# Two of eight K-tile pairs of a feed-forward input by seven block products instead of eight

## What is computed

```python
h = rms_norm(x, ffn_pre_g[l])
gate, up = jnp.split(h @ w_ffn_in[l], 2, axis=-1)
x = x + rms_norm((jax.nn.silu(gate) * up) @ w_ffn_out[l], ffn_post_g[l])
```

## Time and profile before

| | us |
|---|---|
| median of 3 runs (lowest, highest) | 2449.61 (2449.6, 2450.51) |
| span of the profiled execution | 2448.3 |
| one unit of 12 matmuls in the feed-forward input | 2.72 |
| one pair of loop bodies with its transposes | 88.44 |

### The profile page before, as it was taken

One profiled execution on the slowest core, in us unless ns is written; L12 is line 12 of the kernel. 1 busy time (PEld: TensorE's weight loads), 2 busy tenths in 40 slices (PEclk: granted clock), 3 DMA queues, 4 the chain that ended last, 5 costly groups with the idle time before them and its releaser, 6 DMA issues.

```text
span 2448.3 us, 32568 instructions
## 1 busy us (share of the span) xinstructions
PE 2432.0 (99%) x12315; PEld 2031.6 (83%) x12315; DVE 1396.9 (57%) x1987; ACT 1203.4 (49%) x1693; POOL 37.0 (2%) x60
## 2 busy tenths in 40 slices
PE   9999999999999999999999999999999999999998
PEld 7888888887888888888887889898888888888887
DVE  5568888677455555454446436677554554554444
ACT  5665558666444444444345435554544444443443
POOL 1000000000000000000000010000000000000000
PEclk9999999999999999999999999999999999999999
DMA  7765544445655655555556764434555556556554
GB/s 235 243 209 179 167 148 172 165 170 182 197 189 188 195 188 189 191 189 191 196 191 204 220 217 156 143 113 164 180 190 190 189 188 195 189 188 206 194 193 154
DMA packets 233850, 455.80 MB, mean 186 GB/s; under 512 B 16698, under 2 KB 19002, under 8 KB 233232
## 3 DMA queue, kind: packets, MB, share of 16 engines
q1 hardware_dynamic: 227008, 431.49, 54.3%
q0 software_dynamic: 6160, 21.81, 2.6%
q10 hardware_dynamic: 576, 1.05, 0.1%
HBM read 449.04 MB, written 5.24 MB: 186 GB/s over the span
## 4 chain that ended last, share of the span: by engine, by line
PE 96%; DVE 2%; ACT 1%; DMA 1%; issue 0%; SPq 0%; ACTq 0%; DVEq 0%
PE g L312 24%; PE g L314 24%; PE g L313 24%; PE g L1326 4%; PE g L1327 4%; PE g L1328 4%; PE g L2263 1%; PE g L2267 1%; PE g L2265 1%; PE m L829 1%; PE m L1358 1%; PE m L2276 1%; DVE wl L300 1%; PE m L1041 0%; PE m L2348 0%
## 5 line engine op out<-in xcount | busy, mean ns | idle before, releaser
L300 DVE TENSOR_TENSOR wl<-raw,wh 128x1024 fp32r<-128x1024 f32 (+1 forms) x820 | 996.0, 1220 | 920.7 <-ACT wh L296 917.0
L296 ACT ACTIVATE wh<-raw 128x1024 fp32r<-128x1024 f32 (+1 forms) x819 | 860.4, 1056 | 1066.9 <-PE g L314 911.3
L312 PE MATMUL g<-wh,act_hi 128*128 128x512 f32 x1792 | 702.0, 392 | 0.9 <-DVE wl L300 0.5
L314 PE MATMUL g<-wh,act_lo 128*128 128x512 f32 x1792 | 697.7, 389 | 0.0
L313 PE MATMUL g<-wl,act_hi 128*128 128x512 f32 x1792 | 697.4, 389 | 0.0
L312 PEld LDWEIGHTS g<-wh,act_hi 128*128 128x128 f32 x1792 | 336.4, 188 | 73.6 <-issue 2.9
L314 PEld LDWEIGHTS g<-wh,act_lo 128*128 128x128 f32 x1792 | 336.3, 188 | 70.5
L313 PEld LDWEIGHTS g<-wl,act_hi 128*128 128x128 f32 x1792 | 336.5, 188 | 68.7
L312 PE MATMUL g<-wh,ht_hi 128*128 128x512 f32 x672 | 261.6, 389 | 0.0
L314 PE MATMUL g<-wh,ht_lo 128*128 128x512 f32 x672 | 261.4, 389 | 0.0
L313 PE MATMUL g<-wl,ht_hi 128*128 128x512 f32 x672 | 261.4, 389 | 0.0
(11 more groups left out here) (424 smaller groups left out, 2225.6 us busy)
## 6 DMA issues: line engine op xcount, KB each, us to landing
raw<-in_w_ffn_in SPq DMA_DIRECT2D x176, 512.0 KB, 3.5
raw<-in_ffn_w_in SPq DMA_DIRECT2D x176, 512.0 KB, 3.5
raw<-in_w_in SPq DMA_DIRECT2D x111, 512.0 KB, 4.5
raw<-in_w_ffn_out SPq DMA_DIRECT2D x88, 512.0 KB, 3.5
raw<-in_ffn_w_out SPq DMA_DIRECT2D x88, 512.0 KB, 3.6
raw<-in_nsa_w_in SPq DMA_DIRECT2D x80, 512.0 KB, 4.4
raw<-in_w_out SPq DMA_DIRECT2D x32, 512.0 KB, 4.1
raw<-in_nsa_w_out SPq DMA_DIRECT2D x32, 512.0 KB, 4.6
```

The source lines that it names most:

```text
L296: nc.scalar.activation(wh[:, j % SLOTS, 0:n], raw[:, j % SLOTS, 0:n], ACT.Copy).then_inc(hi_done, 1)
L300: nc.vector.tensor_tensor(wl[:, j % SLOTS, 0:n], raw[:, j % SLOTS, 0:n], wh[:, j % SLOTS, 0:n].bitcast(F32), ALU.subtract).then_inc(lo_don ...
L312: nc.tensor.matmul(dst, h, whk, start=(first and k == 0), stop=False)
L314: ins = nc.tensor.matmul(dst, l, whk, start=False, stop=(last and k == 1))
```

## The change

Take two K-tiles of the gate and of the up chunk and the two halves of the rows: that is a product of a 2 x 2 matrix of activation blocks with a 2 x 2 matrix of weight blocks, eight block products. Strassen's scheme (in Winograd's form) needs seven, of sums of blocks. The changed kernel does this for K-tile pairs 1 and 2 of the eight, in every body but the first.

- A body has 20 units in the ring instead of 16 (`FF_NEXT`). Units 2 to 5 and 10 to 13 are a group of seven each (`SEVEN_AT`). Of the four units of a group two are loaded (gate and up of the pair), and two are sums that VectorE writes into the raw slots in three steps (`weight_sums`) before it converts the first unit of the group; no load is issued for them. Of a group's second unit only half is converted. TensorE runs 6, 3, 6 and 6 matmuls on them (`pe_seven`).
- The sums of activations are made once for each layer in the first body, by VectorE in five steps behind unit 11, and split by ScalarE behind unit 12 and VectorE behind unit 13.
- The products of the groups that more than one result needs stand in the four banks of `m`. ScalarE copies one out behind its unit 17, and VectorE adds them up in three steps behind its unit 17 (`shared_sums`), each of which waits for the one before. At the end of a body VectorE adds to the gate banks what is shared (`ff_b`), and ScalarE makes `silu` of that; behind unit 3 of the next body VectorE makes the up rows (`up_rows`) and then the product.
- `m` also takes the transposes. They move from behind unit 7 of an even body to behind unit 16, and TensorE waits for the shared sums before unit 16. The copies out of `m` move from behind unit 11 to the end of the body.
- Units 0, 1, 6 to 9 are the gate's other six pairs, 14 to 19 the up's.
- `g_b` is used for `shared` in the feed-forward input, so GpSimd's load of `ffn_post_g` moves to the end of it.
- Some semaphores are merged: the transpose of the gains waits for three small loads more; a wait for these is left out later.

```diff
...
+SEVENS = 2
+FF_FIRST, FF_NEXT = 16, 20
...
+        GATES, SEVEN_AT, SEVEN_K = {0: 0, 1: 3, 6: 4, 7: 5, 8: 6, 9: 7}, (2, 10), (1, 2)
+        UPS = {14: 3, 15: 4, 16: 0, 17: 5, 18: 6, 19: 7}
+
+        STEPS = {"t2": (1, 3), "rows": 2, "u2": 4, "u34": 5, "shared": 6}
...
+        def pe_seven(pe, name, i, p):
...
+            first, last = p == 0, p == SEVENS - 1
+            converted(0)
+            product(0, 0, *of_x(0, 0), m[:, 0, :], first, last)
+            product(0, 1, *of_x(1, 0), g[:, 0, :], False, last).then_inc(unit_used, 1)
+            converted(1)
+            if first:
+                pe.wait_ge(pair_free[1], s["pair0"][1] + i + 1)
+            product(1, 1, *of_sums(3), g[:, 2, :], first, False).then_inc(unit_used, 1)
+            converted(2)
+            product(2, 0, *of_sums(0), m[:, 2, :], first, last)
+            product(2, 1, *of_sums(2), m[:, 1, :], first, last).then_inc(unit_used, 1)
+            converted(3)
+            product(3, 0, *of_sums(1), m[:, 3, :], first, last)
+            product(3, 1, *of_x(1, 1), g[:, 1, :], False, last).then_inc(unit_used, 1)
...
+            def body(i, par, first):
+                if first:
+                    return opening()
+                for j in range(FF_NEXT):
+                    if j == 0:
+                        pe.wait_ge(pair_free[0], s["pair0"][0] + i + 1)
+                    if j == SEVEN_AT[0]:
+                        if par:
+                            pe.wait_ge(lo_evac, BANKS[name] + 2 * i - 2)
+                        else:
+                            pe.wait_ge(ff_step, ff_stepped(name, i - 1, STEPS["shared"]))
+                    if j == 16 and par == 0:
+                        pe.wait_ge(ff_step, ff_stepped(name, i, STEPS["shared"]))
                         pe.wait_ge(lo_evac, BANKS[name] + 2 * i - 4)
...
+                    if j in SEVEN_AT:
+                        pe_seven(pe, name, i, SEVEN_AT.index(j))
...
+                    if j == 16 and par == 0:
                         pe_ff_turn2(pe)
...
+                for j in range(FF_NEXT):
+                    if j - 1 in SEVEN_AT:
...
+                        nc.scalar.activation(wh[:, j % SLOTS, NB:UE], raw[:, j % SLOTS, NB:UE], ACT.Copy).then_inc(hi_done, 1)
+                    else:
+                        act_unit(act, ff_cyc(s, i), j)
+                    if j == 17:
+                        act.wait_ge(unit_used, ff_used(s, i, 13))
+                        nc.scalar.activation(shared[:, 0, :], m[:, 0, :], ACT.Copy).then_inc(ff_kept, 1)
+                if par == 0:
+                    act_ff_turn2(act, name, i)
+                act.wait_ge(pair_free[0], s["pair0"][0] + i + 2)
+                gated(par, 0)
+                gated(par, 1).then_inc(ff_kept, 1)
...
+            def weight_sums(i, p):
...
+                nc.vector.tensor_tensor(t1_t3, b12_b22, raw[:, j % SLOTS:j % SLOTS + 2, 0:NB], ALU.add).then_inc(raw_full[(j + 2) % SLOTS], 16)
+                dve.wait_ge(raw_full[(j + 2) % SLOTS], (cyc + (j + 2) // SLOTS) * 16 + 16)
+                nc.vector.tensor_tensor(t2_t4[:, 0, :], t1_t3[:, 0, :], b12_b22[:, 1, :], ALU.add).then_inc(ff_step, 1)
+                dve.wait_ge(ff_step, ff_stepped(name, i, STEPS["t2"][p]))
+                nc.vector.tensor_tensor(t2_t4[:, 1, :], t2_t4[:, 0, :], b11_b21[:, 1, :], ALU.add).then_inc(raw_full[(j + 3) % SLOTS], 16)
...
+            def up_rows(i):
+
+                dve.wait_ge(unit_used, ff_used(s, i, FF_NEXT - 1))
+                nc.vector.tensor_tensor(shared[:, T:2 * T, :], g[:, T:2 * T, :], shared[:, T:2 * T, :], ALU.subtract).then_inc(pair_free[1], 1)
+                dve.wait_ge(pair_free[1], s["pair0"][1] + i + 2)
...
+            def shared_sums(i):
...
+                nc.vector.tensor_tensor(shared[:, 3, :], shared[:, 0, :], m[:, 3, :], ALU.add).then_inc(ff_step, 1)
+                dve.wait_ge(ff_step, ff_stepped(name, i, STEPS["u2"]))
+                u2 = shared[:, 3:4, :].broadcast_to([P, 2, NB])
+                nc.vector.tensor_tensor(shared[:, 1:3, :], m[:, 1:3, :], u2, ALU.add).then_inc(ff_step, 1)
+                dve.wait_ge(ff_step, ff_stepped(name, i, STEPS["u34"]))
+                nc.vector.tensor_tensor(shared[:, 3, :], shared[:, 1, :], m[:, 2, :], ALU.add).then_inc(ff_step, 1)
...
+                for j in range(FF_NEXT):
+                    if j in SEVEN_AT:
+                        weight_sums(i, SEVEN_AT.index(j))
+                    if j - 1 in SEVEN_AT:
+                        half_unit(i, j)
+                    else:
+                        dve_unit(dve, ff_cyc(s, i), j)
+                    if j == 3:
+                        up_rows(i - 1)
                         mul(i - 1, 1 - par)
...
+                    if j == 17:
+                        shared_sums(i)
+                if par == 0:
+                    dve.wait_ge(turned, BANKS[name] + 2 * i)
+                nc.vector.tensor_tensor(ff_b[par][:, :, :], g[:, 0:T, :], shared[:, 0:T, :], ALU.add).then_inc(pair_free[0], 1)
+                if par == 0:
+                    dve_ff_turn2(dve, name, i)
...
         def pe_other_gains(pe):
-            pe.wait_ge(gains_in, 16 * 5)
+            pe.wait_ge(tables_in, 16 * 8)
...
-            pool.wait_ge(pair_free[1], gemms["co"]["pair0"][1] + 3)
+            pool.wait_ge(ff_step, ff_stepped("ff1", PAIRS, 1))
             pool.dma_start(g_b[:, :], bcast(a["ffn_post_g"], D)).then_inc(gb_in, 16)
...
```

More of the change, by code:

```diff
@@ new lines, in pe_ff_unit @@
+        def pe_ff_unit(pe, cyc, j, c, u, starts, last):
+            pe.wait_ge(lo_done, SLOTS + (cyc + j // SLOTS) * SLOTS + j % SLOTS + 1)
+            for k in range(2):
+                whk = wh[:, j % SLOTS, k * NB:(k + 1) * NB]
+                wlk = wl[:, j % SLOTS, k * NB:(k + 1) * NB]
+                for t in range(T):
+                    dst = g[:, 2 * c + t, :]
+                    h = act_hi[:, 2 * u + k, t * P:(t + 1) * P]
+                    l = act_lo[:, 2 * u + k, t * P:(t + 1) * P]
+                    nc.tensor.matmul(dst, h, whk, start=(t in starts and k == 0), stop=False)
+                    nc.tensor.matmul(dst, h, wlk, start=False, stop=False)
+                    ins = nc.tensor.matmul(dst, l, whk, start=False, stop=(last and k == 1))
+            ins.then_inc(unit_used, 1)
@@ L1091, in act_ffn_in, with gated @@
             s = gemms[name]
-            def body(i, par, first):
[L1094 to L1106, removed]
+            def gated(par, t):
+                src = ff_b[par] if par is not None else g
+                return nc.scalar.activation(ff_b[par or 0][:, t, :], src[:, t, :], ACT.Silu, scale=rstd(turn)[:, t:t + 1])
@@ new lines, in split_sums, with opening @@
+            def split_sums():
+                dve.wait_ge(ff_summed, 3 * LAYER[name] + 2)
+                nc.vector.tensor_tensor(sums_lo[:, :, :, :], sums[:, :, :, :], sums_hi[:, :, :, :].bitcast(F32), ALU.subtract)\
+                  .then_inc(ff_summed, 1)
+                dve.wait_ge(ff_summed, 3 * LAYER[name] + 3)
+                link_d(dve, nc.vector.memset(shared[:, T:2 * T, :], 0.0))
+            def opening():
+                if turn not in SPLIT:
+                    dve_add_block(dve, turn, 0)
+                for j in range(FF_FIRST):
+                    if j >= AHEAD:
+                        dve_unit(dve, s["u0"] // SLOTS, j)
+                    dve_lead_in(dve, turn, j)
+                    if j == 11:
+                        sums_of_x()
+                    if j == 13:
+                        split_sums()
@@ L1118, in mul @@
                                                          in1=ff_b[par][:, t, :], op0=ALU.mult, op1=ALU.mult)
-                ins.then_inc(pair_free[1], 1)
-            def body(i, par, first):
[L1122 to L1129, removed]
-                        mul(i - 1, 1 - par)
-                    if j == 11 and par == 0 and not first:
-                        dve_ff_turn2(dve, name, i)
+                ins.then_inc(ff_step, 1)
```

161 lines of the change are left out of this document (120 added, 41 removed).

## The result

The changed kernel takes 2466.5 us (median of 4 runs, 2465.95 to 2466.84), the kernel before 2449.74 beside it: ratio 1.0066, 95% interval 1.0054 to 1.0079. It is slower by 16.8 us, where the prediction had 5.8.

A forecast was written before the change was run, and what follows sets the result against it. TensorE alone was taken to set the time. Per pair of bodies, 3.3 us of waiting against 2.72 saved gives +0.58, for ten pairs +5.8: 2449.6 + 5.8 = 2455.4 us, own range 2446 to 2466, outer range 2429 to 2473.

The forecast's parts named there:

- The saving: Feed-forward input: 186 matmuls per body for 192, 1.36 us in each of 20 bodies, 27.2 us in all.
- Rival 4: Groups of seven: products changing banks cost more than plain matmuls; 0.1 us each costs 28 us; 0.17 together with Rival 3.
- Rival 3: VectorE's chain, at units 4 and 16, is longer than its rows: 2 us a pair more, 2475; 0.17 together with Rival 4.
- the mark between the forecast and rival 1: Loads in the loop: median above 4.4 us to landing for the forecast; 3.5 would make rival 1 right.
- rival 1: Loop loads land as if alone, in 3.4 us; only unit 16 waits, 0.94 us: 2431.8; chance 0.30 up to 2445.
- Place (a): Ahead of unit 16 in even bodies, TensorE waits for the shared sums, late by 2.6 us including unit 14's share.
- The floor in it: Ahead of unit 16 in even bodies: late by 0.94 us even if the load takes 3.4 us.
- Place (b): Unit 14: load 11 lands late, delaying weight sums and load 14; 0.1 to 0.2 us in odd bodies.
- Place (c): Unit 4 of an even body: VectorE's chain from the odd body's load 17 makes it late by 0.5 us.
- the restart after each stall: TensorE's restart after stalls, with a group's first product after a bank change: bounded by 0 and 0.3 us per pair.
- The estimate by the rule on the drain of VectorE: Some 12 VectorE steps before unit 4 take 0.09 us more each: 11 us higher, 2466; 0.02 of Rival 3's chance.
- Edits at nothing: First-body sums of x, gain transposes' wait, GpSimd's load, merged semaphores and others: costed at nothing, with their cover.

The follow-up runs named there:

- experiment 4: Against the changed kernel, each feed-forward input load of a unit brings 256 KB instead of 512, so the output is not the result: 2430.02 us, ratio 0.9918.
- experiment 5: Against the changed kernel, VectorE converts a group's first unit before the weight sums, and SyncE's reload of that slot also waits for the sums: 2460.39 us, ratio 1.0040.
- the floor kernel: Against the changed kernel, shared sums behind unit 15 instead of 17 and 256 of 512 columns per load, so output is wrong: 2423.09 us, ratio 0.9890.
- the versions behind unit 15 and 16: Two kernels: the changed kernel with shared sums and ScalarE's copy behind unit 15 (2442.43 us) or unit 16 (2443.54 us) instead of unit 17.
- the best version: Against the changed kernel, shared sums behind unit 15 and a group's first unit converted before the weight sums: 2431.2 us, ratio 0.9922.

## Why the prediction was right and where it was off

**The saving: right.** 27.2 us predicted, 2450.16 - 2423.09 = 27.1 measured. Rival 4 (products dearer than plain ones) is out.

**The sign and the mechanism: right; the size a third of what was measured.** Slower was the likeliest side with 0.42; TensorE has idle time at the three places named, each ended by the step named. But 2466.5 lies half a microsecond above the forecast's own range of 2446 to 2466, in the stretch that was given to rivals 3 and 4 with 0.17; only the outer range, 2429 to 2473, holds it. The loads took 4.5 to 4.6 us, over the 4.4 that I had set as the mark between the forecast and rival 1. Half loads come near the case of rival 1, with 2430.0 for its 2431.8, but they land in 2.9 us and not in its 3.4.

**Place (a), unit 16.** Predicted 2.6 us a pair, with what unit 14 of the even body had given up; measured 1.73 + 0.63 = 2.36. The floor in it is confirmed by experiment 4. What was too large is the burst: I took landing times of 5.0 to 5.7, and load 17 took 4.80 in the median of the ten even bodies (4.55 to 5.46), so 1.4 over a load alone and not 1.6 to 2.3. With the floor of 0.94 that is 2.34. The burst is also less close than I had it: loads 14, 15 and 16 of the chain above went out 3.6, 3.0 and 1.9 us ahead of load 17, not within 2.

**Place (b), unit 14 of the odd body.** Predicted 0.1 to 0.2, measured 0.61. My sum laid VectorE's steps end to end from the moment when load 11 lands; experiment 5 shows that about half of the two waits at unit 14 (0.58 of 1.24) comes from the order in which VectorE takes the weight sums and the conversion behind them. Three terms of my sum were short. The weight sums start 0.25 us after load 11 has landed, and I had nothing there; they hold VectorE for 2.66 and not 2.57; load 14, the first of its burst, took 3.7 and not 3.4. From the landing of load 11 to TensorE's start it is 10.5 us in the median of the ten odd bodies, where I had 9.9. And load 11 landed at 15.5 to 16.6 in the eight pairs, not at 15.1 to 16.1. With half loads the wait is gone.

**Place (c), unit 4.** Predicted 0.5, measured 0.34.

**The sum of the waits: right by cancelling.** 3.3 predicted, 3.32 measured. But a pair took 89.57 and not 89.03. The missing 0.54 a pair, 5.4 us in ten, is the step "the restart after each stall I bound by 0 and 0.3 us per pair" and the choice of nothing for it. A restart costs 0.12 to 0.15 us, 0.10 of it between the first two matmuls, as in the timeline above, and the four places of a pair make 0.54, more than the bound of 0.3. That closes the account: 89.57 - 85.70 = 3.87, and 3.32 + 0.54 = 3.86.

**The first pairs: missed.** I multiplied one pair by ten. The way to the first group of transposes took 6.75 us more than in the floor kernel in the first layer, and 5.65 in the second, against 3.9 for a pair in the loop: 4.6 us together. The worst stall of the kernel is there, and the clock fell behind it (last section). The others are in the first odd body, where the loop has only just begun behind the written-out body:

```profile
647.68 0.50 PE L1149 MATMUL g<-wh,act_hi 128*128 128x512 f32 x1 [1.33 <-DVE wl L308]
1775.08 0.50 PE L1112 MATMUL m<-wh,sums_hi 128*128 128x512 f32 x1 [0.98 <-DVE wl L308]
```

Together: 5.4 + 4.6 + 0.7 (the floor is 2423.1, not 2422.4) = 10.7 of the 11.1 us by which 2466.5 lies above 2455.4.

**Rival 3, the longer chain on VectorE: not the cause, though its 2475 is no farther from the time than my 2455.4.** Steps that wait for their own engine do cost more than the 0.03 that I took (next section), but the versions behind unit 15 and 16 have every one of these steps and are 23 to 24 us faster. The estimate by the rule on the drain of VectorE came to 2466 as well, which is the time measured, but not for its reason. Two conversions in a row still take 2.36 us in the changed kernel's loop (at 788.90), not 2 x 1.23, as in the earlier trace rows. The Trainium skill, page "VectorE: DVE Perf Modes", section "Terms", has the next operation wait until the pipe is empty; the trace disagrees before the change and after it.

**Edits at nothing.** The sums of x in the first body, the gains' transpose and GpSimd's load held (the transpose starts at 47.6 in the earlier trace rows, where the prediction wrote 47.4, which changes nothing): the kernel's other stages keep their lengths within 0.5 us, and in the floor kernel, which has these edits too, nothing is left to be paid for them beyond the 0.7 us.

**What stays open.** The best version is 8.1 us above the floor. Of the eight waits in its view, seven are for a conversion that had itself waited for its load; the longest, 1.3 us ahead of unit 14 in the first even body of the second layer, goes back to a load that took 6.4 us. Whether another order of the loads themselves would get these back wasn't tried.

## What to carry to other kernels

When a change puts derived data into a ring, ask for each added step on the helping engine what it is queued behind: three sums behind one late conversion cost 24 us in this kernel, and the same sums one or two units earlier cost next to nothing. A saving on the bounding engine shortens the cover of every wait at once, so compute the floor (here with loads of half the size) first: it tells how much of the loss is waiting and how much is work, here with the sums moved as well, since half loads alone left 0.6 us a pair. And price waits at neighbouring places together, since slack won at one is handed on to the next that has the same deadline.

## What the runs showed of the hardware

**The clock of TensorE fell once in a stall-ridden stretch, and the length of the last stall doesn't tell when.** I had said that a fall would mean a missed mechanism; it was the stall itself. In the changed kernel it came behind the wait of the first layer's first even body. Windows (length, busy time of PE, PEld, DVE, ACT, POOL, granted clock, DMA share, GB/s), then TensorE's timeline:

```profile
700.00:703.30 3.30, 3.30 (x10) 2.08 (x10) 0.97 (x1) 0.00 (x0) 0.00 (x0) 0.50 0.65 194
703.30:710.00 6.70, 6.70 (x57) 5.69 (x58) 5.28 (x7) 5.18 (x8) 0.00 (x0) 1.00 0.17 63
...
698.73 0.49 PE L1149 MATMUL g<-wh,act_hi 128*128 128x512 f32 x1 [2.50 <-DVE shared L1313]
...
700.50 0.63 PE L1149 MATMUL g<-wh,act_hi 128*128 128x512 f32 x1
700.93 0.63 PE L1150 MATMUL g<-wl,act_hi 128*128 128x512 f32 x1
```

The granted clock is 0.50 (1.2 GHz), and the matmuls are 0.43 us apart instead of 0.23; seven of them at 0.2 more are 1.4 us. The kernel of experiment 5 shows the same once, but not behind its longest stall. Its timeline at the first and the third wait for the shared sums, and the window behind the third:

```profile
697.25 0.49 PE L1151 MATMUL g<-wh,act_hi 128*128 128x512 f32 x1 [2.73 <-DVE shared L1315]
...
875.96 0.49 PE L1151 MATMUL g<-wh,act_hi 128*128 128x512 f32 x1 [1.85 <-DVE shared L1315]
...
876.70:880.10 3.40, 3.40 (x9) 2.65 (x9) 1.50 (x2) 0.00 (x0) 0.00 (x0) 0.51 0.60 191
```

Behind 2.73 us of idling the clock stayed up, behind 1.85 it fell; there unit 14 had stalled for 0.8 us as well, 7.6 us earlier. In the versions without a wait for the shared sums it fell nowhere in the loop. The Trainium skill, page "TensorE: Matmul & The Clock Gate", section "Wait — 56ns, not 53.3ns?", gives 426.7 ns between the starts of matmuls of 512 columns at the lower clock, and the trace agrees; at the upper clock it gives 215.7, where these take 226.7.

**Loads that go out close together land later.** In the loop before, where they go out 2.72 us apart, they took 3.4 us. In the changed kernel a load with no other in flight at its issue took 3.7 us in the median (46 loads), with one 4.35 (147), with two 4.9 (128), with three 5.0 (31). This cost more than anything else (36.5 us by experiment 4, with the size of the loads itself in it), and none of the edits of the order brought the median down (4.6 in the best version); loads of 256 KB took 2.9.

**A step that waits for the step before it on its own engine costs 0.03 us in the kernel before, but up to 0.22 in the loop of the changed kernel.** VectorE's timeline, up rows and the product that waits for them:

```profile
715.20 1.22 DVE L1293 TENSOR_TENSOR shared<-g,shared 128x1024 f32<-128x1024 f32 x1
716.64 1.41 DVE L1300 SCALAR_TENSOR_TENSOR ff_b<-shared,st,ff_b 128x512 f32<-128x512 f32 x2 [0.22 <-DVE shared L1293]
```

In the shared sums it is 0.03 to 0.05. What makes some dearer is open. It isn't only that the awaited count is worked out from the loop's register, since the shared sums await such counts too; ahead of the product the program has three waits.

**Times that hang on loads can scatter.** The kernel before stays within 1.5 us over 16 runs and the floor kernel within 0.8 over 4, but the version behind unit 16 ranges over 9.2 us in 10 runs and the best version over 6.4 in 5. The changed kernel, which waits the most, stayed within 0.9 in its 4 runs, so the waits alone don't make the scatter.
